# Turning half of a gated branch with VectorE and SyncE's moves instead of TensorE, in a two-layer decoder trunk

## The reference, cut to what matters

```python
for l in range(2):                       # S = 256 tokens, D = 1024
    h = rms_norm(x, mix_norm_g[l])
    z = h @ w_in[l]                      # columns: u, v, query latent, kv latent, rotary key, two gates
    # branch A: gelu(u) * (W_s layer_norm(gelu(v)) + b), 8 groups of 128 channels, chunks of 128 tokens
    y_a = gmlp_branch(u, v, ...) @ gm_w_proj[l]
    # branch B: 16 heads of causal attention
    y_b = mla_branch(...) @ mla_w_proj[l]
    x = x + (sigmoid(g_a) * y_a + sigmoid(g_b) * y_b) @ w_out[l]
    x = x + channel_mixer(rms_norm(x))   # dense in layer 0, 8 experts with 2 of 8 taken in layer 1
```

## Time and profile before

| | |
|---|---|
| time, median of 3 runs | 1414.58 us (1413.52 to 1414.61) |
| the profiled execution's own time | 1415.23 us |
| its span in the trace | 1413.5 us |
| TensorE busy | 1404.5 us |
| VectorE busy | 1167.7 us |
| ScalarE busy | 950.0 us |

### The profile page before, as it was taken

The page is one execution under the profiler, slowest core; times in us unless marked ns, Lnnn a source line. Parts: engine busy times, 40 slices in busy tenths (PEclk is TensorE's granted clock), DMA queues, the critical chain, the costliest instruction groups (busy, mean ns, idle before and its releaser), DMA issues.

```text
span 1413.5 us, 19089 instructions
## 1 busy us (share of the span) xinstructions
PE 1404.5 (99%) x6567; PEld 1159.6 (82%) x6567; DVE 1167.7 (83%) x1197; ACT 950.0 (67%) x966; POOL 172.1 (12%) x305
## 2 busy tenths in 40 slices
PE   9999999999999999999999999999999999999998
PEld 7888778888888888788888888888888888888886
DVE  6998766676557899667989898898988988999986
ACT  6678645445435677644777777777777777778774
POOL 2032003476600050000300000000000000000010
PEclk9999999999999999999999999999999999999999
DMA  9476549976666484558999999999999999999995
GB/s 338 163 217 207 179 150 332 300 228 201 200 222 206 155 245 128 194 179 314 330 355 410 365 396 408 373 390 405 351 410 372 385 405 365 393 371 393 409 374 188
DMA packets 171636, 424.32 MB, mean 300 GB/s; under 512 B 19436, under 2 KB 50792, under 8 KB 171544
## 3 DMA queue, kind: packets, MB, share of 16 engines
q1 hardware_dynamic: 157128, 393.42, 76.7%
q0 software_dynamic: 13376, 26.16, 6.1%
q10 hardware_dynamic: 1040, 3.68, 0.6%
HBM read 398.20 MB, written 15.81 MB: 293 GB/s over the span
## 4 chain that ended last, share of the span: by engine, by line
PE 96%; DMA 2%; DVE 1%; ACT 0%; SPq 0%; issue 0%; DVEq 0%; ACTq 0%
PE ps L619 89%; DMA raw_more<-in_moe_w_down 1%; PE ps L1194 1%; PE ps L1053 1%; PE ps L1062 1%; PE ps L932 1%; PE ps L1051 1%; PE ps L1037 1%; PE ps L1010 0%; PE ps L976 0%; DMA raw<-in_w_in 0%; DVE w_lo L554 0%; ACT w_hi L549 0%; PE ps L1035 0%; PE ps L1186 0%; SPq L537 0%
## 5 line engine op out<-in xcount | busy, mean ns | idle before, releaser
L554 DVE TENSOR_TENSOR w_lo<-raw,w_hi 128x2048 fp32r<-128x2048 f32 (+3 forms) x184 | 383.7, 2092 | 78.0 <-ACT w_hi L549 76.9
L549 ACT ACTIVATE w_hi<-raw 128x2048 fp32r<-128x2048 f32 (+3 forms) x184 | 322.2, 1758 | 123.7 <-PE ps L619 97.5
L619 PE MATMUL ps<-w_hi,act_hi 128*128 128x512 f32 (+1 forms) x1264 | 332.4, 391 | 0.6 <-DVE w_hi L1803 0.5
L619 PE MATMUL ps<-w_hi,act_lo 128*128 128x512 f32 (+1 forms) x1264 | 328.5, 387 | 0.0
L619 PE MATMUL ps<-w_lo,act_hi 128*128 128x512 f32 (+1 forms) x1264 | 326.8, 387 | 0.0
L619 PEld LDWEIGHTS ps<-w_lo,act_hi 128*128 128x128 f32 x1264 | 235.8, 188 | 48.2
L619 PEld LDWEIGHTS ps<-w_hi,act_lo 128*128 128x128 f32 x1264 | 235.6, 188 | 48.0
L619 PEld LDWEIGHTS ps<-w_hi,act_hi 128*128 128x128 f32 x1264 | 233.1, 188 | 46.9 <-ACT act_hi L1337 1.2
L554 DVE TENSOR_TENSOR w_lo<-raw_more,w_hi 128x2048 fp32r<-128x2048 f32 (+1 forms) x96 | 201.8, 2110 | 30.4 <-ACT w_hi L549 30.4
L549 ACT ACTIVATE w_hi<-raw_more 128x2048 fp32r<-128x2048 f32 (+1 forms) x96 | 170.0, 1775 | 56.1 <-PE ps L619 46.8
L554 DVE TENSOR_TENSOR w_lo<-raw_low,w_hi 128x2048 fp32r<-128x2048 f32 (+1 forms) x64 | 137.6, 2156 | 13.4 <-ACT w_hi L549 12.7
(11 more groups left out here) (296 smaller groups left out, 1353.3 us busy)
## 6 DMA issues: line engine op xcount, KB each, us to landing
raw<-in_moe_w_gu SPq DMA_DIRECT2D x96, 512.0 KB, 11.7
raw_more<-in_moe_w_down SPq DMA_DIRECT2D x80, 512.0 KB, 10.9
raw<-in_w_in SPq DMA_DIRECT2D x66, 512.0 KB, 5.4
raw_low<-in_moe_w_gu SPq DMA_DIRECT2D x64, 512.0 KB, 12.1
raw_more<-in_moe_w_gu SPq DMA_DIRECT2D x64, 512.0 KB, 12.3
raw<-in_moe_w_gu SPq DMA_DIRECT2D x48, 384.0 KB, 8.4
raw<-in_dense_w_gu SPq DMA_DIRECT2D x34, 512.0 KB, 5.3
raw_lent<-in_moe_w_gu SPq DMA_DIRECT2D x32, 512.0 KB, 11.3
```

The costliest lines, as they stand in the source:

```text
L549: nc.scalar.activation(w_hi[:, self.split_slot(j), 0:n], self.raw(j)[:, 0:n], ACT.Copy).then_inc(self.hi, 1)
L554: nc.vector.tensor_tensor(w_lo[:, c, 0:n], self.raw(j)[:, 0:n], w_hi[:, c, 0:n].bitcast(F32), ALU.subtract).then_inc(self.lo, 1)
L619: return nc.tensor.matmul(dst, a, b, start=start and n == 0, stop=stop and n == 2)
```

## The change

In both layers half 0 of branch A is no longer turned by TensorE. ScalarE writes half 0 of the token product into vbuf in an order by blocks (four 128 by 256 pieces as before, the first now waits for both banks). `branch` for half 0 is eight operations on 128 by 128 instead of two on 128 by 512, and stands behind a split of weights in the chunk u 1 0. SyncE then issues 16 DMAs from vbuf into half 0 of u_buf, each 32 partitions by two runs of 512 bytes. They stand in its queue in front of the load of the chunk that comes four behind u 1 4 on the list of chunks. `a_blocks` turns the moved data in one VectorE operation on 128 by 1024 into a part of kb that is free by then. `a_hi` is the rounded part on ScalarE, two operations on 128 by 512, and `a_lo` the low part on VectorE, two operations on 128 by 512. Three neighbours change place: a_lo stands behind `values` of pair 1, and behind it now first come the maxima of pair 3, then the split of pa 0 0, then the division of pair 3, then the split of pa 0 4. Half 1 stays as it was.

```diff
+        if (what, j, k0) == ("u", 1, 4):
+            moves_at[len(chunks) + 3] = l
...
-        mul(l, "u", 0, 4, [("u_arg", l, 0), split("split_hi"), ("blocks", l, "k", 0), ("u_gelu", l, 0), ("branch", l, 0)],
+        mul(l, "u", 0, 4, [("u_arg", l, 0), split("split_hi"), ("blocks", l, "k", 0), ("u_gelu", l, 0)],
             split=False)
-        mul(l, "u", 1, 0, [*slot(1, exps=False), ("split_lo", l, len(chunks) - 2), split("split_hi")], split=False)
-        mul(l, "u", 1, 4, [("u_square", l, 1), *slot(2, exps=False), ("u_arg", l, 1), ("softmax", l, 1)], split=False,
-            inside=[(2, ("a_turns", l, 0)), (2, ("softmax", l, 0)), (2, ("last_q", l, "q", 1)),
+        mul(l, "u", 1, 0, [*slot(1, exps=False), ("split_lo", l, len(chunks) - 2), ("branch", l, 0), split("split_hi")], split=False)
+        mul(l, "u", 1, 4, [("u_square", l, 1), *slot(2, exps=False), ("u_arg", l, 1), ("a_blocks", l, 0), ("softmax", l, 1)], split=False,
+            inside=[(2, ("softmax", l, 0)), (2, ("last_q", l, "q", 1)),
                     (5, ("split_lo", l, len(chunks) - 2)), (5, split())])
-        mul(l, "gb", 1, 0, [("values", l, 0), split("split_hi"), *slot(3, values=False, exps=False), ("u_gelu", l, 1),
+        mul(l, "gb", 1, 0, [("values", l, 0), ("a_hi", l, 0), split("split_hi"), *slot(3, values=False, exps=False), ("u_gelu", l, 1),
                             ("branch", l, 1), ("blocks", l, "k", 1)], split=False, inside=[(4, ("u_tanh", l, 1))])
-        mul(l, "gb", 1, 4, [("values", l, 1), ("split_lo", l, len(chunks) - 2), *slot(4, values=False, exps=False), split("split_lo"), ("softmax", l, 3), evac("gb", 1)], split=False,
+        mul(l, "gb", 1, 4, [("values", l, 1), ("a_lo", l, 0), *slot(4, values=False, exps=False), ("split_lo", l, len(chunks) - 2), ("softmax", l, 3), split("split_lo"), evac("gb", 1)], split=False,
...
+            def move_branch(l):
+                sp.wait_ge(branch_a, 2 * l + 1)
+                for b in range(4):
+                    for c in range(4):
+                        sp.dma_start(branch_moved[32 * c:32 * c + 32, 0, :, b, :, :],
+                                     branch_by_block(0)[32 * b:32 * b + 32, :, c, :, :]).then_inc(a_moved[0], 16)
...
+                if n in moves_at:
+                    move_branch(moves_at[n])
                 static_load(n)
...
+                        if blocked:
+                            pe.wait_ge(a_hi, BY_BLOCKS * l + k0 // 4 + 1)
...
+                        elif p == 1 and not cell and blocked:
+                            pe.wait_ge(a_lo, BY_BLOCKS * l + k0 // 4 + 1)
...
+                elif kind == "a_hi":
+                    j = step[2]
+                    act.wait_ge(a_turned, BY_BLOCKS * l + j + 1)
+                    for t in range(TT):
+                        op = copy(t1_hi[:, 4 * j:4 * j + 4, t * P:(t + 1) * P].rearrange("p k (b i) -> p k b i", b=4),
+                                  branch_by_tile[:, t].rearrange("p b k i -> p k b i"))
+                    op.then_inc(a_hi, 1)
...
+                elif kind == "a_blocks":
+                    j = step[2]
+                    dve.wait_ge(a_moved[j], 16 * 16 * (l + 1))
+                    if not j:
+                        dve.wait_ge(k_moved[1], 16 * 4 * DG * (l + 1))
+                    nc.vector.transpose(branch_turned, u_buf[:, j].rearrange("p t n -> p (t n)")).then_inc(a_turned, 1)
+                elif kind == "a_lo":
+                    j = step[2]
+                    dve.wait_ge(a_hi, BY_BLOCKS * l + j + 1)
+                    for t in range(TT):
+                        k, cols = slice(4 * j, 4 * j + 4), slice(t * P, (t + 1) * P)
+                        op = tt(t1_lo[:, k, cols].rearrange("p k (b i) -> p k b i", b=4),
+                                branch_by_tile[:, t].rearrange("p b k i -> p k b i"),
+                                t1_hi[:, k, cols].bitcast(F32).rearrange("p k (b i) -> p k b i", b=4), ALU.subtract)
+                    op.then_inc(a_lo, 1)
```

More of the change, by code:

```diff
@@ L132, in decoder_trunk @@
     keys_in = {}
+    moves_at = {}
     def mul(l, what, j, k0=0, then=(), split=True, inside=()):
@@ L381, in decoder_trunk @@
         kb = sb("kb", [P, TT, DG, H, 32], F32, mixer)
+        branch_moved = u_buf[:].rearrange("p j t n -> p j (t n)").rearrange("p j (t b k i) -> p j t b k i", t=TT, b=4, k=4)
+        branch_turned = kb[:].rearrange("p t g h d -> p (t g h d)")[:, 4 * STRIP:6 * STRIP]
+        branch_by_tile = branch_turned.rearrange("p (t b k i) -> p t b k i", t=TT, b=4, k=4)
         vv = sb("vv", [P, TT, H, DV], F32, mixer)
@@ L469, in decoder_trunk @@
         gelu_sq, gelu_arg, gelu_tanh = sem("gelu_sq"), sem("gelu_arg"), sem("gelu_tanh")
+        a_moved, a_turned, a_hi, a_lo = (
+            [sem(f"a_moved{j}") for j in range(1)], sem("a_turned"), sem("a_hi"), sem("a_lo"))
         v_normed, ws_masked, branch_a = sem("v_normed"), sem("ws_masked"), sem("branch_a")
@@ L625, in three, with branch_by_block @@
             return nc.tensor.matmul(dst, a_hi, b_lo, start=False, stop=stop)
+        BY_BLOCKS = 1
+        def branch_by_block(j):
+            return vbuf[:, :, j * STRIP:(j + 1) * STRIP].rearrange("p t (c k i) -> p t c k i", c=4, k=4)
         def turns_in(step):
@@ L672, in operand_turns @@
                     "ukv": lambda: last_turn["latent_turns", l, 1],
-                    "pa": lambda: last_turn["a_turns", l, half],
+                    "pa": lambda: None if half < BY_BLOCKS else last_turn["a_turns", l, half],
                     "pb": lambda: last_turn["values", l, 4 * half + 3],
@@ L1070, in _ @@
                     tiles_first = (what, j, k0) == ("wo", 1, 4)
+                    blocked = what == "pa" and not j and k0 // 4 < BY_BLOCKS
                     if not first:
+                        if blocked:
+                            pe.wait_ge(a_hi, BY_BLOCKS * l + k0 // 4 + 1)
                         if operand is not None:
@@ L1448, in _ @@
                             gg = 4 * step[2] + 2 * b + g
[L1449 to L1452, removed]
-                        op.then_inc(turn_free[bb % 2], 1)
+                            if step[2] < BY_BLOCKS:
+                                if not b and not g:
+                                    act.wait_ge(turn_done, bb + 2)
+                                dst, src = branch_by_block(step[2])[:, :, :, 2 * b + g, :], "p (t c i) -> p t c i"
+                                src = ps[:, 4 + bb % 2, g * S:(g + 1) * S].rearrange(src, t=TT, c=4)
+                            else:
+                                dst = vbuf[:, :, gg * P:(gg + 1) * P]
+                                src = ps[:, 4 + bb % 2, g * S:(g + 1) * S].rearrange("p (t d) -> p t d", t=TT)
+                            op = nc.scalar.activation(dst, src, ACT.Identity, bias=b_sp[:, l, gg:gg + 1], scale=0.5)
+                        op.then_inc(turn_free[bb % 2], 1)
+                elif kind == "a_hi":
[5 more added lines that the diff above has]
+                    op.then_inc(a_hi, 1)
                 elif kind == "values":
@@ L1939, in _ @@
                     for t in range(TT):
-                        op = stt(vbuf[:, t, cols], u_buf[:, j, t, :], mix_scale[:, ONE, t:t + 1], vbuf[:, t, cols],
-                                 ALU.mult, ALU.mult)
-                    op.then_inc(branch_a, 1)
+                        if j < BY_BLOCKS:
+                            for k in range(4):
+                                v = branch_by_block(j)[:, t, :, k, :]
+                                op = stt(v, u_buf[:, j, t, k * P:(k + 1) * P].rearrange("p (c i) -> p c i", c=4),
+                                         mix_scale[:, ONE, t:t + 1], v, ALU.mult, ALU.mult)
+                        else:
+                            op = stt(vbuf[:, t, cols], u_buf[:, j, t, :], mix_scale[:, ONE, t:t + 1], vbuf[:, t, cols],
+                                     ALU.mult, ALU.mult)
+                    op.then_inc(branch_a, 1)
+                elif kind == "a_blocks":
[13 more added lines that the diff above has]
+                    op.then_inc(a_lo, 1)
                 elif kind in ("u_arg", "u_gelu"):
```

## The result

The changed kernel takes 1428.31 us (median of 5 runs, 1425.62 to 1428.93); the kernel before took 1414.58 beside it. The ratio is 1.009, with a 95% interval of 1.0076 to 1.0104. I had forecast 1416.1 and a range from 1413.0 to 1419.2. It is slower by 13.7 us, far outside of it.

What follows compares the result with a forecast made beforehand. TensorE was taken as the bound, VectorE as the near second limit. The transposes' 0.87 us gain is lost; waits of 0.45 and 0.3 cost 0.75 a layer, 1.5 in both, added to 1414.58: 1416.1 us, range 1413.0 to 1419.2.

Steps and rivals of the forecast that it cites:

- the one on the moves: SyncE's 16 moves from 126.3 in layer 0: 0.37 us each, the last issued at 131.9, all landed at 134.4.
- W: How much later than 134.4 the moves come at a_blocks in layer 0; forecast as 0.
- 0.35 + W a layer: TensorE's loss with late moves, from W = 0.4 on, as its two waits don't add up.
- Rival B: The moves are late and VectorE stands at a_blocks: 1419.1 us, or 1423.1 at the longest landing; chance 0.25.
- Landing: Time for SyncE's moves to land: 2.5 us taken, from GpSimd's moves of 1.6 to 5.1, median 3.1.
- VectorE's queue up to a_blocks: VectorE's work until half 1's u_arg: branch 2.2 us, end at 134.4, 0.45 us late, TensorE waiting 0.2 in u 1 4.
- VectorE's order for itself: TensorE's loss from VectorE's lateness with no late moves: 0.75 us a layer.
- The 0.45 at the turns of pair 1: TensorE's turns of pair 1 resume at 137.54, not 137.09, as the low values read the bank 0.45 us late.
- the third pass of pa 0 0: TensorE waits there for VectorE's split, done at 151.35 and wanted about 151.05: another 0.3 us.
- The load of pa 0 4: SyncE's load behind the moves: issued at about 132.3 instead of 129.1, needed after 142, hidden by 10 us.
- Rival A: TensorE's time for half 0's transposes is simply gained: 1.74 us, at most 2.6, 1412.0 to 1412.9; chance 0.12.

Runs made afterwards that it cites:

- The filler: The changed kernel with 36 transposes of the identity on TensorE in front of the wait for the probabilities of pair 1: 1422.49 us.
- the late order: The changed kernel with a_blocks behind half 1's branch, a_hi behind half 1's turns, and more VectorE work put later, including half 0's branch: 1417.63 us.

## Why the prediction was wrong

**The step that failed** is the one on the moves: "With fewer bytes and an empty queue I take 0.37, with bounds of 0.33 and 0.46." It measured 0.60 for the issue and 0.64 to 0.67 from one to the next, beyond my upper bound. The nearest rows, moves from HBM, were taken for moves within SBUF; the experiment from HBM shows that they are cheaper, 0.43. And I argued that fewer bytes would make an issue cheaper; half the bytes left it at 0.59. The last move was issued at 136.5, not 131.9, and W, the time by which the moves come late, was about 4 us and not 0 (VectorE stood for 4.08).

**The term that was missing** is the clock. For a late move I had 0.35 + W a layer, so 4.4 us at this W. Measured are 6.5. The difference of about 2 us is what the lower clock took: from 140.87 to the end of the seven matmuls before half 1's transposes TensorE needed 6.9 us, where it needed 4.6 before (136.41 to 140.97). The filler confirmed it: with the clock kept it needed 4.2. Rival B named the right place, the wait behind a_blocks, and its threshold (W above 1.1) was passed. But it had the moves late by SyncE's longest issues and by the landing, and the typical issue was too slow. Its top of 1423.1 had W at 3.9, which was nearly met, and nothing for the clock; that the measured 1428.3 lies 5 us higher is mostly the clock's part in both layers.

**Landing**: I took 2.5 us and it was 1.9 at the median; the last move of layer 0, issued at 136.5, had landed by 138.44. This helped by 0.6 us.

**VectorE's queue up to a_blocks** was right: branch 2.18 us for 2.2, u_arg's end at 134.36 for 134.4, the wait for w_lo in u 1 4 seen (the third pass began at 124.33 for my 124.1 or 124.2).

**VectorE's order for itself**, 0.75 us a layer by my sum, is about 0.15. The 0.45 at the turns of pair 1 was 0.2 to 0.3; TensorE shows there a wait of 0.6 us for the division, in front of the bank that I had named. In the kernel with two queues the third pass of pa 0 0 lost 0.1 where I had 0.3. And I overlooked that the new place of the split of pa 0 4 lets the low values of pair 2 come 0.5 us earlier, which removes the old wait at pair 3's turns. With that corrected, the change without late moves is neutral, as two kernels measured.

**The load of pa 0 4** I called hidden by 10 us. In the changed kernel VectorE's wait covers it, since all is late together. Without that wait it costs 1.4 us in layer 0. My 10 us ran from an issue at 132.3 to the need at 142, and left out the load itself, 5.2 us: less than 5 were hidden. And it was issued at 137.2 to 139.2.

**Rival A**, the gain of TensorE's 0.87 us, is refuted in all the orders tried. They reached 0.5 to 0.6 us ahead and gave it back. That no order reaches it is not shown; the late order with the moves on two queues is untried.

No version tried beats the kernel before. The best of the new form, with the moves on two queues, can't be told from it: 1414.47 beside 1414.65.

## What to carry to other kernels

A row of small DMAs has a price by its count at the engine that issues them, here the same with 16 KB or 32 KB in each: multiply it before the data, and spread the row over the queues that are idle. Ask of a wait on a queue not only what stands behind it there, but also which load stands behind the moves that it waits for. And price a wait of TensorE with the clock behind it: here 4.6 us without a matmul cost 2 to 3 us more, in matmuls at half the clock.

## What the runs showed of the hardware that I had not expected

- SyncE needed 0.60 us to issue one of these DMAs from SBUF to SBUF over 32 partitions, with 16 KB or with 32; 0.43 at the median from HBM in the same shape. GpSimd needed 0.54 for the same move. The Trainium skill's page "DMA: Bandwidth & Descriptors" (Issuing engine by pattern) calls the path of SyncE and ScalarE generally the faster; for the issue of this form the trace has the opposite by a tenth. For the landing the traces don't settle it: it was 1.9 us at the median with all moves on SyncE and 4.1 with all on GpSimd, but there the load for pa 0 4 was issued in the midst of them; side by side in the kernel with two queues it was 2.9 and 2.5.
- After 4.6 us without a matmul the granted clock was 0.50 for more than 6 us, though TensorE was busy again for nearly all of them. After 3.0 us without one (moves from HBM) it was 0.50 too, for some 3 us. 36 transposes of the identity kept it at 1.00, though 1.8 us without a matmul followed them.
